# Summing expert pairs on TensorE in the last stage, and matmuls without a reader in TensorE's waits, in a diffusion backbone step

## What is computed

```python
out = (ga * y_a + gb * y_f + gc * y_p) @ w_out
x = layer_norm(alpha * x + gate1 * out, ln1_g, ln1_b)
u2 = x * (1 + scale2) + shift2
# each token: best of 4 groups, best 2 of its 4 experts, weights e_w (softmax)
hid = silu(u2 @ w_up_a) * (u2 @ w_up_b)          # of the token's two experts
y = e_w[0] * hid0 @ w_down0 + e_w[1] * hid1 @ w_down1
x = layer_norm(alpha * x + gate2 * y, ln2_g, ln2_b)
```

## Time and profile before

| quantity | value |
|---|---|
| median of 3 runs | 1093.69 us (1093.43 to 1093.86) |
| the profiled execution's own time | 1094.95 us |
| its span, first to last instruction | 1092.9 us |
| mean granted TensorE clock, share of full speed | 0.926 |
| TensorE matmul busy | 954.1 us (87%) |
| VectorE busy | 693.4 us (63%) |
| ScalarE busy | 447.6 us (41%) |
| GpSimd busy | 209.2 us (19%) |

### The profile page before, as it was taken

The page is one execution under the profiler, slowest core; times in us unless marked ns, Lnnn a source line. Parts: engine busy times, 40 slices in busy tenths (PEclk is TensorE's granted clock), DMA queues, the critical chain, the costliest instruction groups (busy, mean ns, idle before and its releaser), DMA issues.

```text
span 1092.9 us, 13352 instructions
## 1 busy us (share of the span) xinstructions
PE 954.1 (87%) x4543; PEld 759.6 (70%) x4543; DVE 693.4 (63%) x966; ACT 447.6 (41%) x616; POOL 209.2 (19%) x217
## 2 busy tenths in 40 slices
PE   7898999999999999599988962799999999999700
PEld 2698998477777777466666752688888888888600
DVE  5887570044343745745679567576899964899367
ACT  2622220234353433302140021556888764688331
POOL 2116401111000001001117351110101010100066
PEclk9898989999999999899998975799999999999955
DMA  9973550333030206514280053795999976999551
GB/s 338 341 269 131 192 175 11 119 104 71 27 114 2 77 1 250 173 39 145 58 289 19 39 197 131 258 393 173 403 398 399 399 259 236 340 399 355 186 218 77
DMA packets 84695, 213.20 MB, mean 195 GB/s; under 512 B 6896, under 2 KB 7174, under 8 KB 84656
## 3 DMA queue, kind: packets, MB, share of 16 engines
q1 hardware_dynamic: 66000, 149.45, 37.6%
q0 software_dynamic: 14512, 48.51, 12.9%
q10 hardware_dynamic: 4144, 14.72, 3.5%
HBM read 189.54 MB, written 23.11 MB: 195 GB/s over the span
## 4 chain that ended last, share of the span: by engine, by line
PE 74%; DVE 14%; ACT 4%; DMA 4%; issue 2%; POOL 1%; ACTq 0%; POOLq 0%; DVEq 0%
PE ps L1922 28%; PE ps L1692 21%; PE ps L1580 7%; PE ps L1678 5%; PE ps L1807 2%; PE ps L1914 2%; PE ps L1746 1%; DMA R_d<-in_w_mod 1%; ACT w_hi L831 1%; DMA R_m<-in_ln_b 1%; PE ps L1801 1%; PE ps L1796 1%; PE ps L1949 1%; DVE ring L1558 1%; PE ps L1590 1%
## 5 line engine op out<-in xcount | busy, mean ns | idle before, releaser
L1692 PE MATMUL ps<-w_hi,uT_hi 128*128 128x512 f32 x320 | 132.8, 415 | 4.3 <-ACT R_x L896 2.5
L1692 PE MATMUL ps<-w_lo,uT_hi 128*128 128x512 f32 x320 | 126.8, 396 | 0.0
L1152 DVE TENSOR_TENSOR w_lo<-ring,w_hi 128x1024 fp32r<-128x1024 f32 x52 | 61.7, 1221 | 33.7 <-ACT w_hi L831 32.7
L1391 DVE TENSOR_TENSOR wa_lo<-ring,wa_hi 128x1024 fp32r<-128x1024 f32 x64 | 74.1, 1220 | 4.4 <-ACT wa_hi L948 4.0
L1692 PEld LDWEIGHTS ps<-w_hi,uT_hi 128*128 128x128 f32 x320 | 61.0, 191 | 21.9 <-issue 5.2
L1692 PEld LDWEIGHTS ps<-w_lo,uT_hi 128*128 128x128 f32 x320 | 60.9, 190 | 13.6
L1922 PE MATMUL ps<-wa_hi,xgT_hi 128*128 128x512 f32 x152 | 62.7, 413 | 5.2 <-DVE xgT_lo L1498 5.2
L738 POOL COPY idx_now<-tile_idx 128x1 int32 (+1 forms) x19 | 12.2, 640 | 285.6 <-PE ps L1914 262.8
L896 ACT ACTIVATE R_x<-ps 128x512 f32<-128x512 f32 x30 | 17.9, 596 | 116.8 <-PE ps L1692 116.8
L1692 PE MATMUL ps<-w_hi,uT_lo_a 128*128 128x512 f32 x160 | 64.5, 403 | 0.0
L1692 PE MATMUL ps<-w_hi,uT_lo_b 128*128 128x512 f32 x160 | 62.3, 390 | 0.0
(11 more groups left out here) (400 smaller groups left out, 2292.6 us busy)
## 6 DMA issues: line engine op xcount, KB each, us to landing
ring<-in_w_up SPq DMA_DIRECT2D x64, 512.0 KB, 8.6
ring<-in_w_in SPq DMA_DIRECT2D x11, 2048.0 KB, 10.2
R_d<-in_w_up SPq DMA_DIRECT2D x32, 512.0 KB, 10.8
R_p<-in_w_down SPq DMA_DIRECT2D x32, 512.0 KB, 9.6
R_h<-in_w_down SPq DMA_DIRECT2D x32, 512.0 KB, 10.2
y_slots<-R_m ACTq DMA_DIRECT2D x19, 512.0 KB, 6.3
ring<-in_w_mod SPq DMA_DIRECT2D x8, 1024.0 KB, 14.2
R_s<-in_w_up SPq DMA_DIRECT2D x16, 512.0 KB, 10.3
```

Source lines behind the costliest of these rows:

```text
L1152: tt(lo[:, at], weights(name)[:, at], hi[:, at].bitcast(F32), ALU.subtract).then_inc(S["w_split"], 1)
L1391: tt(w_hi_lo[i][1][:, at], stage(i, q), w_hi_lo[i][0][:, at].bitcast(F32), ALU.subtract).then_inc(S["up_split"], 1)
L1692: i = mm(out, parts(k)[a][:, tok(j)], w[b][:, k], start=(k == 0 and a + b == 0), stop=(k == KD - 1 and b == 1))
```

## The change

Two things are changed.

The tail. ScalarE makes ten 128x128 diagonal matrices from the pair weights. For each token tile TensorE multiplies the two gathered rows by their diagonals, both into one PSUM sum, with four f32 products of 512 columns, into banks 4 and 5 or 6 and 7 in turn. VectorE multiplies the sum by `gate2` out of PSUM, adds the residual with a row sum as a second output, and makes the negative mean. ScalarE squares the centred tile with a row sum as second output, and takes the root with the scale 1/D and a bias column. VectorE's `finish` does the rest: reciprocal, centre and gain in one pass, scale and bias in another. GpSimd's two passes per tile and `norm_stats` go. The last tile is finished and stored in two halves.

The products without a reader. `idle_products(n)` multiplies the identity with 512 constant columns in f32 into bank 7, `n` times. It stands five times: 7 ahead of `route(4)`, 8 after it, 5 after `rank`, 9 after `slots`, and 9 after the last down product. Only the first has a wait of its own, for VectorE's reading of output tile 3, which used bank 7.

The diff, without the semaphores' list and the helper `out_rows` (the output rows of tile `j`):

```diff
--- before.py
+++ after.py
@@ -406,6 +406,8 @@
         den = cols(H)
         b_r = cols(20)
         w12 = cols(10).rearrange("p (s j) -> p s j", s=2)
+        row_sum, neg_mean, sq_sum, eps_col = cols(NT), cols(NT), cols(NT), cols(1)
+        route_diag = R_m[:, 0:2 * NT * P].rearrange("p (s j t) -> p s j t", s=2, j=NT)
         pool_scratch = cols(1)
         scratch1 = cols(4)
         tile_idx = sb("tile_idx", [P, MAXT], I32)
@@ -758,11 +763,6 @@
                                                  in_offset=bass.IndirectOffsetOnAxis(ap=slot_idx[:, s * NT + j:s * NT + j + 1], axis=0)
                                                  ).then_inc(pair_loaded[j], 16)
 
-            for j in range(NT - 1):
-                pool.wait_ge(S["f_norm"], j + 1)
-                chain(nc_t(x_tok[:, j], x_tok[:, j], ROW2["g2"], ALU.mult))
-                nc_t(x_tok[:, j], x_tok[:, j], ROW2["b2"], ALU.add).then_inc(S["f_ready"], 1)
-
 
         @block.scalar
         def _(act):
@@ -1029,27 +1029,23 @@
             act.wait_ge(S["y_stored"], total * 16 + 1)
             nc.scalar.copy(scratch1[0:1, 3:4], const("one")[0:1, :]).then_inc(S["experts_done"], 1)
 
-            def scale_first(j):
-
-                act.wait_ge(pair_loaded[j], 32)
-                yp = y_pair[j][:, 0]
-                nc.scalar.activation(yp, yp, ACT.Copy, scale=w12[:, 0, j:j + 1]).then_inc(S["y1_scaled"], 1)
-            scale_first(0)
+            act.wait_ge(S["weights_ready"], 1)
             for j in range(NT):
-                if j + 1 < NT:
-                    scale_first(j + 1)
-                act.wait_ge(S["f_var"], j + 1)
-                nc.scalar.activation(rstd[:, j:j + 1], rstd[:, j:j + 1], ACT.Sqrt).then_inc(S["f_std"], 1)
-                act.wait_ge(S["f_pre"], j + 1)
-                nc.scalar.activation(x_tok[:, j], x_tok[:, j], ACT.Identity, bias=shift_mean[:, j:j + 1],
-                                     scale=rstd[:, j:j + 1]).then_inc(S["f_norm"], 1)
+                for s_ in range(2):
+                    nc.scalar.mul(route_diag[:, s_, j], ident, w12[:, s_, j:j + 1]).then_inc(S["diag_ready"], 1)
+            for j in range(NT):
+                act.wait_ge(S["f_mean"], j + 1)
+                nc.scalar.activation(y_pair[j][:, 1], x_tok[:, j], ACT.Square, bias=neg_mean[:, j:j + 1],
+                                     accum_out=sq_sum[:, j:j + 1]).then_inc(S["f_squared"], 1)
+                act.wait_ge(S["f_squared"], j + 1)
+                nc.scalar.activation(rstd[:, j:j + 1], sq_sum[:, j:j + 1], ACT.Sqrt, scale=1.0 / D, bias=eps_col).then_inc(S["f_std"], 1)
                 if j:
                     act.wait_ge(S["f_ready"], j)
-                    dst = y_prompt[0] if j == 1 else y_sample[0, (j - 2) * P:(j - 1) * P, :]
-                    act.dma_start(dst, x_tok[:, j - 1]).then_inc(S["out_stored"], 16)
-            act.wait_ge(S["f_ready_last"], 1)
-            act.dma_start(y_sample[0, (NT - 2) * P:(NT - 1) * P, :], x_tok[:, NT - 1]).then_inc(S["out_stored"], 16)
-            act.wait_ge(S["out_stored"], 16 * NT)
+                    act.dma_start(out_rows(j - 1), x_tok[:, j - 1]).then_inc(S["out_stored"], 16)
+            for n in range(2):
+                act.wait_ge(S["f_ready"], NT + n)
+                act.dma_start(out_rows(NT - 1)[:, n * BW:(n + 1) * BW], x_tok[:, NT - 1, n * BW:(n + 1) * BW]).then_inc(S["out_stored"], 16)
+            act.wait_ge(S["out_stored"], 16 * (NT + 1))
             act.wait_ge(S["states_stored"], 16 * 6)
 
 
@@ -1545,29 +1541,27 @@
                 expert_tile(s)
             expert_tile(last, last=True)
 
+            ch(nc.vector.memset(eps_col, EPS))
             dve.wait_ge(S["rows2_loaded"], 16 * 4)
             def finish(j):
 
                 dve.wait_ge(S["f_std"], j + 1)
                 ch(nc.vector.reciprocal(rstd[:, j:j + 1], rstd[:, j:j + 1]))
-                stt(shift_mean[:, j:j + 1], mv[:, 2 * j:2 * j + 1], -1.0, rstd[:, j:j + 1], ALU.mult, ALU.mult).then_inc(S["f_pre"], 1)
+                ch(stt(x_tok[:, j], x_tok[:, j], neg_mean[:, j:j + 1], ROW2["g2"], ALU.add, ALU.mult))
+                for at in ([slice(0, BW), slice(BW, D)] if j == NT - 1 else [slice(0, D)]):
+                    stt(x_tok[:, j, at], x_tok[:, j, at], rstd[:, j:j + 1], ROW2["b2"][:, at], ALU.mult, ALU.add).then_inc(S["f_ready"], 1)
             for j in range(NT):
-                yp = y_pair[j]
-                dve.wait_ge(pair_loaded[j], 32)
-                dve.wait_ge(S["y1_scaled"], j + 1)
-                ch(stt(yp[:, 0], yp[:, 1], w12[:, 1, j:j + 1], yp[:, 0], ALU.mult, ALU.add))
+                yp, b0 = y_pair[j][:, 0], 4 + 2 * (j % 2)
+                dve.wait_ge(S["f_combined"], j + 1)
+                tt(yp.rearrange("p (b n) -> p b n", b=2), ps[:, b0:b0 + 2, :],
+                   ROW2["gate2_0" if j == 0 else "gate2_1"].rearrange("p (b n) -> p b n", b=2), ALU.mult).then_inc(S["f_gated"], 1)
+                dve.wait_ge(S["f_gated"], j + 1)
+                stt(x_tok[:, j], x_tok[:, j], ALPHA, yp, ALU.mult, ALU.add, accum_out=row_sum[:, j:j + 1]).then_inc(S["f_summed"], 1)
+                dve.wait_ge(S["f_summed"], j + 1)
+                ts(neg_mean[:, j:j + 1], row_sum[:, j:j + 1], -1.0 / D, None, ALU.mult).then_inc(S["f_mean"], 1)
                 if j:
                     finish(j - 1)
-                ch(tt(yp[:, 0], yp[:, 0], ROW2["gate2_0" if j == 0 else "gate2_1"], ALU.mult))
-                stt(x_tok[:, j], x_tok[:, j], ALPHA, yp[:, 0], ALU.mult, ALU.add).then_inc(S["f_summed"], 1)
-                dve.wait_ge(S["f_summed"], j + 1)
-                norm_stats(x_tok[:, j], j)
-                ts(rstd[:, j:j + 1], mv[:, 2 * j + 1:2 * j + 2], EPS, None, ALU.add).then_inc(S["f_var"], 1)
             finish(NT - 1)
-            jl = NT - 1
-            dve.wait_ge(S["f_norm"], NT)
-            ch(tt(x_tok[:, jl], x_tok[:, jl], ROW2["g2"], ALU.mult))
-            tt(x_tok[:, jl], x_tok[:, jl], ROW2["b2"], ALU.add).then_inc(S["f_ready_last"], 1)
 
 
         @block.tensor
@@ -1879,6 +1873,10 @@
                 i = product(bank(1)[:, j * 20:(j + 1) * 20], "lg", lambda k: u2T[:, j % 2, k], lambda k: w_r[:, k], KD)
                 if j == NT - 1:
                     filled(i, "lg")
+            def idle_products(n):
+
+                for _ in range(n):
+                    mm(bank(7), ident, consts[:, 0:BW], start=True, stop=True)
             for j in range(NT):
                 name = ("out", j)
                 begin(pe, name)
@@ -1887,7 +1885,10 @@
                 filled(i, name)
                 if j:
                     route(j - 1)
+            was_read(pe, ("out", NT - 2))
+            idle_products(7)
             route(NT - 1)
+            idle_products(8)
 
             pe.wait_ge(S["masks_ready"], 1)
             begin(pe, "rank")
@@ -1898,12 +1899,14 @@
             mm(bank(0)[:, 0:NT * NE], ones, before_all[:, 0:NT * NE], start=False, stop=True)
             i = mm(bank(0)[:, NT * NE:(NT + 1) * NE], ones, before_all[:, NT * NE:], start=True, stop=True)
             filled(i, "rank")
+            idle_products(5)
 
             begin(pe, "slots")
             for n_ in range(2 * NT):
                 pe.wait_ge(S["onehots"], 2 + n_ + 1)
                 i = mm(bank(1)[:, 0:MAXT], hot_place[:, n_], hot_tile[:, n_], start=(n_ == 0), stop=(n_ == 2 * NT - 1))
             filled(i, "slots")
+            idle_products(9)
 
             for n_ in ("rank", "slots", ("uT2", NT - 1, 0), ("uT2", NT - 1, 1), ("out", 4), ("out", 3)):
                 was_read(pe, n_)
@@ -1963,6 +1966,17 @@
                                start=(k == 0 and a + b == 0), stop=(k == KF - 1 and a == 1))
                     if k == KF - 1:
                         i.then_inc(S["down_full"], 1)
+            idle_products(9)
+            pe.wait_ge(S["diag_ready"], 2 * NT)
+            for j in range(NT):
+                pe.wait_ge(pair_loaded[j], 32)
+                if j >= 2:
+                    pe.wait_ge(S["f_gated"], j - 1)
+                for n in range(2):
+                    for s_ in range(2):
+                        i = mm(bank(4 + 2 * (j % 2) + n), route_diag[:, s_, j], y_pair[j][:, s_, n * BW:(n + 1) * BW],
+                               start=(s_ == 0), stop=(s_ == 1))
+                i.then_inc(S["f_combined"], 1)
 
 
 _INS = ["x_prompt", "x_sample", "c", "state_C", "state_n", "state_m", "c_ctx", "ln_in_g", "ln_in_b", "w_mod", "b_mod",
```

More of the change, by code:

```diff
@@ L428, in backbone @@
             "abs_ready", "act_chain", "bmod_loaded", "mod_acc", "consts_rest", "gates_placed", "x_spilled4", "posr_loaded", "pos_loaded", "gb_row_loaded", "plan_ready", "cleared", "consts_loaded", "dexp",
-            "down_full", "dve_chain", "exp_cond", "experts_done", "f_ready", "f_pre", "y1_scaled", "f_summed", "f_norm", "f_ready_last", "rows1_folded", "scale2_ready",
-            "f_std", "f_var", "fine_exp", "gathered", "gb_loaded", "hT_full",
```

(4 more changed lines are left out.)

## The result

| quantity | before | after |
|---|---|---|
| median (lowest to highest), 4 runs each | 1093.78 us (1093.43 to 1093.92) | 1077.83 us (1077.01 to 1082.19) |
| ratio, 95% interval | | 0.9861 (0.9835 to 0.9887) |
| profiled execution: time, span | 1094.95, 1092.9 us | 1078.64, 1076.8 us |
| mean granted clock | 0.926 | 0.964 |

The account below looks back on a forecast made before the run. TensorE waiting for VectorE at reduced clock ahead of the experts, and VectorE in the tail, were taken as bounds; 8.5 (tail) plus 2.25 (ahead of the experts), 10.7 us off the median, gave 1083.0 us, range 1079.3 to 1086.7.

Parts of the forecast that it names:

- GpSimd's queue loses its passes and gets nothing: Tail: GpSimd's two passes per tile go and no work replaces them; no gain was priced for the end of its program.
- Splitting that store … I count nothing: Last store: issuing it in two halves gains at most part of 2.6 us; counted as nothing.
- The 0.2%: Measurement: a difference of about 0.2% (2.2 us) can be told from no change.
- The tail's 8.5: Tail: 9.3 us earlier last store, less 0.8 for half a clock fall; 8.5 us saved, ends 6.5 and 10.
- Ahead of the experts, 2.25: Before the expert tiles: 0.55 from `route(4)`, 0.9 from transposes, 0.8 from the experts' start; 2.25 us saved, ends 0 and 4.5.
- The `route` term: `route(4)`: running at full clock keeps at most 1.1 us, or zero if the clock falls again; 0.55 taken.
- `slots`' nine products: After `slots`: nine products take 7.7 us, or 9.4 with a fall; loss between nothing and 1 us, taken as nothing.
- C: Rival, tail: Square and Sqrt each need table loads on every tile, 1.3 us later on the last; 1084.3 us, chance 0.08.
- E: Rival, tail: TensorE's sum saves nothing, only the 2.25 us ahead of the experts remain; 1091.4 us, chance 0.02.
- A: Rival: clock holds at `route(4)`, the experts' start and the tail; 13.7 us off, 1080.0 us, chance 0.17.
- B: Rival: clock falls at every gap, nine products end 0.5 late; 7.65 us off, 1086.0 us, chance 0.13.
- D: Rival: idle products run at half clock, 1.71 us each, and hold TensorE up; 18 us slower, 1112 us, chance 0.03.

Follow-up runs that it names:

- e3: Changed kernel plus one late GpSimd sum of one column that nobody reads, waiting until tile 3 is finished: 1080.55 us.
- e7: Changed kernel with the last tile finished in one pass and stored by one DMA instead of halves: 1082.52 us, one execution.
- e4: Changed kernel with products without a reader in three more gaps and 12 instead of 9 ahead of the tail's sums: 1072.69 us.
- e6: Changed kernel with 12 instead of 9 products without a reader after `slots`: 1083.83 us, one execution.
- e8: Changed kernel with e4's four edits, and 7 instead of 5 products after `rank`, 8 instead of 9 after `slots`: 1074.35 us.
- e5: The changed kernel run again, unaltered, for its spread: 1080.49 us, ratio 0.9889 to the kernel before.

## Why the prediction was wrong, and where it was right

The bottlenecks and the mechanisms were those forecast; the sum missed the end of the program. Of the spans' difference of 16.03, 10.75 was forecast; the 5.28 that were missed are 2.52 at the end (F), 0.83 ahead of the experts, 0.12 in the tail and 1.81 in A.

- **The step that failed: "GpSimd's queue loses its passes and gets nothing."** Priced at nothing, it was worth 1.9 us (e3), because GpSimd's drain, 7.1 us after its last instruction, ended the kernel before. I followed the chain to the last store and took everything after it as the same. The rows already showed it: the earlier trace rows has the last store issued at 1087.88, has such a store landing in 2.6, which makes 1090.5, and the span is 1092.9. Of the 2.4 us between, after keeps some 0.4 (F is 2.46, its last half lands in 2.1); the rest has no owner in the page.
- **"Splitting that store … I count nothing":** 0.6 (e7). The last half lands in 2.1 where the whole took 2.6. Together 2.5 us; with them the sum is 13.25 off, 1080.4, inside the range and beside the repeat's 1080.49.
- **Chance:** 1.8 us of the first result lie in A, which no edit touches; without them it would be about 1079.6, just inside the range. Over all ten profiles A goes from 585.9 to 592.3. The 0.2% that I said a measurement can tell was too fine: the three runs shown then agreed within 0.43 us, the eight of after are 6 us apart.
- **The tail's 8.5:** 8.62 measured; that the two are so near is luck, since two errors cancel. A tile takes 5.30 on VectorE and not 5.6, 1.2 us better over four tiles: the second output costs 0.08 (bounds 0 and 0.2), and the two small instructions of a block take 0.26 from start to start where three of 0.2 were counted. The last `finish` with its issue is a little longer than its 2.75 (E would be 8.84 by these two terms and is 8.62). The clock, on the other hand, did fall: the second sum came 8.76 after the first pair, where 7.1 was forecast for full clock, so the fall took 1.66 and not half of it; e4, which bridges the gap, has E 1.62 shorter. The wait for TensorE was at the second tile alone, as forecast.
- **Ahead of the experts, 2.25:** 3.08. The transposes gave 0.9 and the experts' start 0.8, both as forecast, with the fall after 2.46. The `route` term was halved between 1.1 and 0; after shows 27.30 − 26.07 = 1.23, e6 and e8 (27.12 in both) show 0.18 when a fall inside the seven products makes them late. Both cases that I averaged exist; an execution has one or the other.
- **`slots`' nine products, "between nothing and 1 us of loss":** nothing in after and e5 (0.57 and 0.55 left before the transposes), about 2.5 lost in e4's execution. The short fall that the bound allowed for did come in after (9.67 for the nine). The bound was too tight for e4, which shows ten microseconds at half clock.
- **Rivals.** C is false here: Square ran at 1049.58 before the only load (1050.83), and again at 1052.91 after the root without one. The Trainium skill (ScalarE: Activation LUTs, Table sets: the hidden batching unit) does not list it among the functions that are in every set. In this trace it ran under the set that was there before that load and under the one that the load brought. E is false (stage E is 8.62 shorter); of what stood against it, the collisions with GpSimd are the larger part by the rows of the kernel before. A, every gap bridged, is what e4 and e8 come near to, by more products than the change has. B's falls happened behind the three gaps, but its late groups did not in after. D decided one group of e4.

## What to carry to other kernels

Before taking the end of a program as fixed, add the last store's landing time to its issue and compare with the span; where time is left, look at which engine finished last, and keep GpSimd's last instruction well ahead of the last store. Where GpSimd runs passes beside VectorE, compare a block of VectorE's work with and without them before judging what bounds it. Products without a reader give back a fall of TensorE's clock (1.6 us each here) only if they leave no open gap of the size that falls in the same trace, and a group must be short enough to fit when it runs at half speed, since the next work waits for what it overruns. Where an untouched stretch varies more than the effect, read the effect stage by stage between fixed starts.

## What the runs showed of the hardware

- GpSimd's drain at the end of its program ended 7.1 us after its last instruction, whether that was a pass of 2.34 us or a sum of one column of 0.19. Behind the last pair gather it was 8.9 in after (1046.96 to 1055.83), where nothing waited for it.
- While a GpSimd pass ran, VectorE's line 1553, on one column, took 1.98 and ended with the pass (1062.70 and 1062.69); without one it took 0.16.
- The clock fell after idle gaps of 2.46, 2.75 and 2.85 in after, but not after 2.46 in e6. After the gap of 2.2 ahead of `slots` it fell at once in e4 and only inside the nine products in after; in e8, with no gap there, it stayed up. It stayed up in e4 where products left 0.74 (experts' start), 0.32 (last expert tile) and 0.27 (tail).
- Ten small ACTIVATEs took 3.02, 0.30 each, against 0.37 in the earlier trace rows, hidden as assumed.
- A stretch that no edit touches (A) varied by 6.4 us between profiles.
